# Where the high and low parts of weights lie in SBUF: seven places 16 bytes apart within 512, in a two-block float32 kernel

## The reference

```
x = x + 0.5 * swiglu_ffn(x, ffn1_norm, ffn1_w_gate, ffn1_w_up, ffn1_w_down)
(aq, ak, av, iq, ik, iw, mx, mv, mi, mf, mo, ga, gb) = split_columns(rms_norm(x, mix_norm) @ w_in)
ya = dsa_attention(...)          # top-64 of at most 256 keys, by an index score
yb = mlstm_branch(...)
x = x + (sigmoid(ga) * (ya @ w_proj_a) + sigmoid(gb) * (yb @ w_proj_b)) @ w_out
x = x + 0.5 * swiglu_ffn(x, ffn2_norm, ...)
# second block
x = x + 0.5 * rmsnorm(swiglu(rmsnorm(x, ...), ...), ...)
x = x + rmsnorm(concat(moba_attention(...), multiscale_pool(...)) @ w_out_2, ...)
x = x + rmsnorm(memory_cross_attention(rmsnorm(x, ...), rmsnorm(mem, ...), wq, wkv, wo), ...)
x = x + 0.5 * rmsnorm(swiglu(rmsnorm(x, ...), ...), ...)
```

## Time and profile before

| | |
|---|---|
| median of 3 runs | 1120.89 us (1120.57 to 1121.79) |
| span of the profiled execution | 1114.4 us |
| TensorE busy | 1104.9 us (99%), 7560 matmuls |
| VectorE busy | 720.3 us (65%) |
| ScalarE busy | 562.5 us (50%) |
| GpSimd busy | 51.3 us (5%) |
| read from HBM | 206.98 MB, 187 GB/s over the span |

### The profile page before, as it was taken

How to read it: one execution, slowest core, us unless ns; L and a number is a source line. 1 busy time by engine, 2 the same in 40 slices (tenths; PEclk the granted TensorE clock), 3 DMA queues, 4 the chain that set the end, 5 groups by cost and what they waited for, 6 DMA issues and landing times.

```text
span 1114.4 us, 17847 instructions
## 1 busy us (share of the span) xinstructions
PE 1104.9 (99%) x7560; PEld 1007.3 (90%) x7560; DVE 720.3 (65%) x833; ACT 562.5 (50%) x743; POOL 51.3 (5%) x63
## 2 busy tenths in 40 slices
PE   8999999999999999999999999999999999999998
PEld 6999988988999899998889998889988987999986
DVE  7865644788967666664475666555868657666652
ACT  7554443467664454444444545445746446444441
POOL 0000000300000000000020000010201001000000
PEclk9999999999999999999999999999999999999999
DMA  8857655754465576666487576539355635766641
GB/s 279 295 176 212 193 175 137 224 164 135 126 197 165 176 247 188 203 183 201 133 287 222 156 245 187 187 119 346 114 170 175 204 114 179 237 188 191 199 141 38
DMA packets 112607, 209.19 MB, mean 188 GB/s; under 512 B 8848, under 2 KB 18192, under 8 KB 112400
## 3 DMA queue, kind: packets, MB, share of 16 engines
q1 hardware_dynamic: 109728, 198.53, 56.9%
q0 software_dynamic: 2512, 9.44, 2.6%
q10 hardware_dynamic: 288, 0.08, 0.0%
HBM read 206.98 MB, written 1.05 MB: 187 GB/s over the span
## 4 chain that ended last, share of the span: by engine, by line
PE 96%; DVE 2%; issue 1%; ACT 0%; DMA 0%; POOL 0%; DVEq 0%; POOLq 0%; ACTq 0%
PE pair L453 93%; PE pair L457 3%; DVE w_lo L1440 1%; DMA ident<-in_consts 0%; DVE xr L1466 0%; DVE x L1579 0%; DVE h_lo L1499 0%; POOL stat L2088 0%; ACT xr L1050 0%; ACT r_hi L1062 0%; DVE r_lo L1477 0%; POOL post_stat L2092 0%; ACT xr L1044 0%; DVEq L2181 0%; DVE y L1571 0%
## 5 line engine op out<-in xcount | busy, mean ns | idle before, releaser
L1440 DVE TENSOR_TENSOR w_lo<-stage,w_hi 128x1024 fp32r<-128x1024 f32 (+2 forms) x376 | 455.7, 1227 | 214.2 <-ACT w_hi L1038 212.1
L1038 ACT CAST w_hi<-stage 128x1024 fp32r<-128x1024 f32 (+2 forms) x376 | 387.2, 1045 | 290.2 <-PE pair L453 279.9
L453 PE MATMUL pair<-h_hi,w_hi 128*128 128x256 f32 x1504 | 418.2, 278 | 0.0
L453 PE MATMUL pair<-h_hi,w_lo 128*128 128x256 f32 x1504 | 416.0, 277 | 0.0
L453 PE MATMUL pair<-h_lo,w_hi 128*128 128x256 f32 x1504 | 415.9, 277 | 0.0
L453 PEld LDWEIGHTS pair<-h_hi,w_hi 128*128 128x128 f32 x1504 | 282.5, 188 | 4.3 <-issue 3.1
L453 PEld LDWEIGHTS pair<-h_hi,w_lo 128*128 128x128 f32 x1504 | 282.7, 188 | 0.0
L453 PEld LDWEIGHTS pair<-h_lo,w_hi 128*128 128x128 f32 x1504 | 282.4, 188 | 0.2
L453 PE MATMUL pair<-w_hi,f_hi 128*128 128x512 f32 x352 | 137.7, 391 | 0.0
L453 PE MATMUL pair<-w_lo,f_hi 128*128 128x512 f32 x352 | 137.1, 389 | 0.0
L453 PE MATMUL pair<-w_hi,f_lo 128*128 128x512 f32 x352 | 137.0, 389 | 0.0
(11 more groups left out here) (289 smaller groups left out, 941.4 us busy)
## 6 DMA issues: line engine op xcount, KB each, us to landing
stage<-in_ffn_w_up SPq DMA_DIRECT2D x88, 512.0 KB, 4.4
stage<-in_ffn_w_down SPq DMA_DIRECT2D x88, 512.0 KB, 3.9
stage<-in_ffn_w_gate SPq DMA_DIRECT2D x87, 512.0 KB, 4.4
stage<-in_w_in SPq DMA_DIRECT2D x52, 512.0 KB, 4.2
stage<-in_w_out SPq DMA_DIRECT2D x16, 512.0 KB, 4.0
stage<-in_xa_wkv SPq DMA_DIRECT2D x16, 512.0 KB, 5.0
stage<-in_xa_wq SPq DMA_DIRECT2D x8, 512.0 KB, 4.5
stage<-in_xa_wo SPq DMA_DIRECT2D x8, 512.0 KB, 5.6
```

The costliest lines, as they stand in the source:

```text
L453: return e.matmul(o, l, r, start=start, stop=stop, skip_group_check=True)
L1038: e.copy(m.w_hi[u % PLACES][:, 0:w], m.stage[u % STAGES][:, 0:w]).then_inc(s.hi, 1)
L1440: e.tensor_tensor(m.w_lo[slot][:, 0:w], m.stage[u % STAGES][:, 0:w], m.w_hi[slot][:, 0:w].bitcast(F32), ALU.subtract).then_inc(s.lo, 1)
```

## The change

The seven high parts are now slices of one tile, and so are the seven low parts. A slice begins 1028 float32 after the one before, 4112 bytes, so that each starts 16 bytes further within 512. The tile starts at 384 modulo 512, and the first slice 4 float32 into it, at 400; the others at 416, 432, 448, 464, 480 and 496. Only place 3 is where all were. Each tile is a little longer than its seven parts were (28,912 bytes against 28,672). Of what lies behind, all that has a rest of its own moves by whole multiples of 512; `ident`, `causal`, `stat` and `pre_gain` move by 192 modulo 512 (`ident` from 96 to 288), and so do `y` and the feed-forward buffers `act_buf2` and `act_rows2` (288 to 480). No instruction is added, removed or moved on any engine.

```diff
         self.stage = [sb(f"stage{i}", [P, UNIT]) for i in range(STAGES)]
-        self.w_hi = [sb(f"w_hi{i}", [P, UNIT], F32R, W_REST) for i in range(PLACES)]
-        self.w_lo = [sb(f"w_lo{i}", [P, UNIT], F32R, W_REST) for i in range(PLACES)]
+        step, first = 4, -12
+        self.w_hi, self.w_lo = [], []
+        for name, places in (("w_hi", self.w_hi), ("w_lo", self.w_lo)):
+            row = sb(name, [P, PLACES * (UNIT + step) + 32], F32R, W_REST - 64)
+            for i in range(PLACES):
+                at = 16 + first + i * (UNIT + step)
+                places.append(row[:, at:at + UNIT])
```

## The result

The changed kernel takes 1146.00 us (median of 3 runs, 1144.82 to 1146.30) against 1120.89. The ratio is 1.0227, with a 95% interval from 1.0209 to 1.0245. I had forecast 1126.2, with a range up to 1137: right in sign, and five times too small in size.

What follows compares the result with a forecast made beforehand. TensorE's matmul spacing was taken to bound the kernel. Cols blocks 3.9 and rows on f 1.4, all else 0, made 5.3 us: span 1114.4 to 1119.7, plus 6.5 around it, time 1126.2 us; range 1114.5 to 1137.

Steps and rivals of the forecast that it cites:

- What bounds the kernel: TensorE, busy 1104.9 of 1114.4 us: how fast matmuls follow each other; operand distance and stream entry cost 0 to 6 ns.
- The writers: ScalarE's cast and VectorE's subtraction, now writing at shifted starts: costed at 0, means of 1045 and 1227 ns to hold.
- Transposes: TensorE's transposes, the largest group streaming ident: 0, as ident is 32 bytes off a multiple of 64 before and after.
- The cols blocks: 3840 matmuls streaming h past weights outside the mixers: four outer places slow 40% of the time, by 4.5 ns, 3.9 us.
- My own upper bound: Cols blocks outside the mixers: six places of seven fall into the slow beat, 4.5 ns each on 3840 matmuls, 14.8 us.
- Rows on f: 1056 matmuls streaming weights past f: four outer places cost 2.3 ns each, 1.4 us; upper bound 2.1 us.
- Rows on h: 960 rows matmuls on h, r and mem, already paying 2.3 ns: taken as 0, since shifts go both ways.
- What lies around the span: Time outside the profiled span, median 1120.89 against span 1114.4: 6.5 us, which the change doesn't touch.
- Extra fetches: Rival, chance 0.14: streamed weights in rows blocks touch 33 pieces of 64 bytes, not 32; 12.3 us more, time 1133.
- No change: Rival, chance 0.22: stream entry decides the beat, fast distances reach beyond 48 bytes either side; within 2 us of 1120.9.
- Faster: Rival, chance 0.28: changing distances push slow streams into the fast beat, mixers' cols and rows on h; 4.4 us, time 1116.5.

Runs made afterwards that it cites:

- 432: As a kernel: all fourteen weight places at 432 modulo 512, against the changed kernel's seven different places; 1148.55 us, ratio 1.0267.
- 452: All fourteen weight places at 452, one float32 behind 448, against the changed kernel's seven different places; 1155.75 us, ratio 1.0338.
- 444: All fourteen weight places at 444, one float32 before 448, against the changed kernel's seven different places; 1140.99 us, ratio 1.0217.
- the move by 32: Weights, h and f all moved by 32 bytes against the kernel before, distances between operands unchanged; 1116.40 us, ratio 0.9993.

## Why the prediction was wrong

*What bounds the kernel.* Right: the loss is all in TensorE's spacing, with no new wait. That addresses set this spacing was right too, but partly by luck. The difference of 276 and 281 ns on which the argument rested has one and the same distance, 320, on both sides, so it couldn't show that a distance matters; only the rows of other pairs hinted at it.

*The writers, 0.* Right: 1226 and 1044 ns.

*Transposes and all others, 0.* Right: +0.3 us.

*The cols blocks, 3.9 us.* This step failed: it measured 22.3 us. I took the slow beat of the first mixer for something that shifted places would fall into now and then, "as often as the first mixer's stretches do, 40%", and left the two places 16 bytes off fast. But the two beats of before, 113.4 and 117.8, are both beats of the distance 320, of which one execution takes the one and another the other, as the kernel before run again shows. The fast one exists at that distance alone among the five I tried as one for all (256, 304, 316, 320, 324). So no shifted place was spared, and in place of 4/7 and 0.40 it should have been 6/7 and 1. Place 3 did stay fast (113.7 ns in the feed-forwards), as I had said. My own upper bound, 14.8 us, was too low too, for two reasons. It took the slow beat's price, 4.5 ns, as the highest, while the shifted places cost 3.9 to 8.6 ns (117.3 at 480 to about 122 at 432, by recorded starts, the units at entries included, against 113.4). And it gave the mixers nothing, though their fast stretches were lost too. All 4896 matmuls went from 114.7 to 119.3 ns, gaps at entries included.

*Rows on f, 1.4 us of at most 2.1.* Measured 5.1. The bound came from the distance to h, +2.3 ns, the nearest row; other shifts cost up to 10 ns (432, 452), which no row of before showed. In the rows on f here, place by place and by recorded starts, it is 0.6 ns (432) to 7.6 (400), and 3.2 at 448 itself.

*Rows on h, 0.* Measured +2.2; they had a better beat to go to (388 ns at 444), but also worse ones (404 at 452), and seven mixed places land on the bad side.

*What lies around the span, 6.5 us.* Wrong as well: the profiled execution of the changed kernel took 1146.3 us with a span of 1144.3, so 2.0 us lie around it, and 1.8 to 3.3 in every run of the experiments. The other 4.5 are most likely chance: the profiled execution of before would belong to the lower of the two groups of times, and its median of 3 to the upper. That would also be why the spans differ by 29.9 us and the medians by 25.1.

*The rivals.* Extra fetches, 1133 us, fell with the move by 32. Its sign, rows on f of 395 ns or more, was all but met (394 to 396), so that sign couldn't tell it from a price of the distance. "No change" supposed a band of distances wider than 48 bytes, and fell with one float32 of shift. "Faster" took the slow beat for a thing that a change of distance would shake off; the kernel with all places 64 bytes apart shows the reverse, as the unit at 448 caught a slow beat among its neighbours, 117.9 ns. The rule of the Trainium skill by which I had put the sum at 0, in "TensorE: Matmul & The Clock Gate", section "Step-by-step: what each phase is for", independent read ports and no loss from loading the next weights, doesn't hold in this case's runs: moving h against the weights, with no other operand of the cols blocks changed, cost 25.7 us at 144 and 28.6 at 192. The rows that I had set against it, 276 and 281, didn't yet contradict it.

What stays open: why 320 and not 304 or 256; whether 512 is the period or only a multiple of it; what rules the rows blocks; what picks the beat of a stretch. That the two reads of TensorE get in each other's way is the reading that fits, but no run looked inside them.

## What to carry to other kernels

In a kernel bound by float32r matmuls, treat the start addresses of the streamed and the stationary operand as one parameter, to the element: keep both on 16 bytes, sweep their distance modulo 512, and then give every buffer of a rotation exactly the same place within 512, since one product of three off it slows the other two. Where a trace shows one form of matmul with two mean durations at a full clock and without waits, that is a beat, and the fast one may hang on an address. Bound the price of an untried address by more than the nearest row: by recorded starts it went from -2 (rows on h at 444) to +11 ns a matmul (rows on h at 452).

## What the runs showed that I had not expected

One float32 of shift costs 24 us in 1117 (444), or 39 (452). A distance can have two beats, 113.4 and 117.8 ns, of which one execution takes the one and another the other, for 864 matmuls in a row; one program's time spreads by 1% on one chip (1114.0 to 1124.9 us in 23 runs), for which a few such picks would be enough, while the kernel with weights and h 16 further and f at 448, whose cols blocks were all fast in its profiled execution, spread over 1117.8 to 1119.6 in 12. A single profiled execution of such a kernel is a draw; by my estimate, from 3.8 us for one feed-forward, two spans of one execution each can't be compared below some 5 us.
